# Last stage on token rows: x turned during routing, the gate folded into the expert rows, skips of the extra turns nested

## The reference

```python
g_idx = argmax(h @ w_rg + b_rg); p_group = softmax(...)[g_idx]        # one of 4 groups per token
top_v, top_i = top_k(expert logits of that group, 2)                   # 2 of its 8 experts
gate = p_group * softmax(top_v)                                        # two weights per token
y = (silu(xb @ w_g[e]) * (xb @ w_u[e])) @ w_d[e]                       # D 1024 -> 512 -> 1024, 32 experts
f = sum over the token's two experts of gate * y
x = x_mid + g2 * f                                                     # g2: one factor per feature
return rmsnorm(x, final_norm)                                          # x / sqrt(mean(x^2) + eps) * final_norm
```

## Time and profile before

| | us |
|---|---|
| median of 3 runs | 2240.37 (2237.33 to 2245.26) |
| the profiled execution | 2240.0, its span 2238.2 |
| PE busy | 1921.9 (86%) |
| DVE busy | 886.4 (40%) |
| ACT busy | 378.0 (17%) |
| mean granted clock of PE | 0.923 of full speed |
| DRAM read and written | 359.09 MB, 16.78 MB |

### The profile page before, as it was taken

One profiled execution on the slowest core, in us unless ns is written; L12 is line 12 of the kernel. 1 busy time (PEld: TensorE's weight loads), 2 busy tenths in 40 slices (PEclk: granted clock), 3 DMA queues, 4 the chain that ended last, 5 costly groups with the idle time before them and its releaser, 6 DMA issues. The chain is left out here.

```text
span 2238.2 us, 27833 instructions
## 1 busy us (share of the span) xinstructions
PE 1921.9 (86%) x12018; PEld 997.4 (45%) x12018; DVE 886.4 (40%) x1460; ACT 378.0 (17%) x666; POOL 127.9 (6%) x185
## 2 busy tenths in 40 slices
PE   6999663998699999999898999999996988777882
PEld 3554353886344444444344664456433333332331
DVE  2572575344314888883442004934313000000003
ACT  4212531223102111111012001035012000000001
POOL 0000007230000000000000000010000000000000
PEclk8999875899799999999999999999997999999985
DMA  7452011112211222215641132220445999999973
GB/s 292 158 194 104 0 40 34 27 23 88 91 40 73 75 75 76 75 58 192 275 190 57 57 99 85 75 86 16 159 173 223 425 427 426 426 426 425 425 334 122
DMA packets 72738, 371.84 MB, mean 166 GB/s; under 512 B 33488, under 2 KB 33616, under 8 KB 46240
## 3 DMA queue, kind: packets, MB, share of 16 engines
q1 hardware_dynamic: 68000, 361.21, 41.2%
q0 software_dynamic: 4608, 8.73, 1.0%
HBM read 359.09 MB, written 16.78 MB: 168 GB/s over the span
## 5 line engine op out<-in xcount | busy, mean ns | idle before, releaser
L2467 PE MATMUL psum<-mem 128*64 128x512 f32 x1536 | 364.1, 629 | 53.0 <-DMA mem<-in_w_upe 29.4
L1604 PE MATMUL psum<-mem 128*128 128x512 f32 x704 | 305.7, 596 | 2.0 <-ACT mem L376 2.0
L1331 PE MATMUL psum<-mem 128*128 128x512 f32 x608 | 274.5, 607 | 20.0 <-DMA mem<-in_w_down 14.7
L2467 PEld LDWEIGHTS psum<-mem 128*64 128x64 f32 x1536 | 121.7, 144 | 274.2 <-issue 268.3
L1673 DVE SCALAR_TENSOR_TENSOR mem<-mem 128x512 f32<-128x512 f32 x352 | 237.0, 749 | 0.0
L1837 PE MATMUL psum<-mem 128*128 128x512 f32 x512 | 223.2, 597 | 2.9 <-ACT mem L1851 2.9
L1604 PEld LDWEIGHTS psum<-mem 128*128 128x128 f32 x704 | 134.0, 191 | 173.1 <-issue 171.6
L1331 PEld LDWEIGHTS psum<-mem 128*128 128x128 f32 x608 | 115.2, 193 | 165.5 <-issue 153.5
L568 PE MATMUL psum<-mem 128*128 128x512 f32 (+1 forms) x464 | 167.6, 523 | 2.1 <-ACT mem L376 2.0
L1837 PEld LDWEIGHTS psum<-mem 128*128 128x128 f32 x512 | 97.5, 191 | 125.6 <-issue 123.1
L568 PEld LDWEIGHTS psum<-mem 128*128 128x128 f32 x464 | 88.1, 190 | 80.8 <-issue 73.0
(11 more groups left out here) (342 smaller groups left out, 1995.0 us busy)
## 6 DMA issues: line engine op xcount, KB each, us to landing
mem<-in_w_gate SPq DMA_DIRECT2D x32, 2048.0 KB, 33.3
mem<-in_w_upe SPq DMA_DIRECT2D x32, 2048.0 KB, 32.7
mem<-in_w_downe SPq DMA_DIRECT2D x32, 2048.0 KB, 32.4
mem<-in_ada SPq DMA_DIRECT2D x48, 1024.0 KB, 6.6
mem<-in_w_up SPq DMA_DIRECT2D x22, 1024.0 KB, 4.8
mem<-in_w_in_g SPq DMA_DIRECT2D x12, 1024.0 KB, 4.8
mem<-in_w_down SPq DMA_DIRECT2D x16, 704.0 KB, 4.2
mem<-in_w_in SPq DMA_DIRECT2D x19, 512.0 KB, 3.7
```

The costliest lines, as they stand in the source:

```text
L1331: last = pe.matmul(self.banks[m % 4][:, :], w, self.rhs[:, kt], start=i == 0, stop=i == n - 1, skip_group_check=self.before is not None)
L1604: last = pe.matmul(k.bank[2 * (m % 3) + h2][:, :], w[:, kt, h2], h[:, kt], start=kt == 0, stop=kt == KD - 1)
L2467: last = pe.matmul(bank[halves[h], :], xs[:, kt, halves[h]], pair[h][0][:, kt, cols], start=kt == 0, stop=kt == tiles - 1, skip_group_chec ...
```

## The change

The kernel's output becomes [512 tokens, 1024 features] instead of feature-major, and the constant final_norm is loaded as a [128, 1024] tile of equal rows (final_row) instead of 8 columns of the first constants tile, which shrinks from 860 to 852 columns, so every tile behind it lies 32 bytes lower in each partition.

In routing, PE turns x in place behind the table products, ACT copies it back, and a row of g2 on all partitions (gate_row) is made from eight diagonal tiles:

```diff
             last.then_inc(s["table_mm"], 1)
+            for i in range(8):
+                if i == 2:
+                    pe.wait_ge(s["rows"], 4)
+                if i >= 4:
+                    pe.wait_ge(s["x_rows"], i - 3)
+                for j in range(4):
+                    last = pe.transpose(k.bank[x_banks[i % 4]][:, P * j:P * j + P], halves_of_x[i][:, j], k.c("ident"))
+                last.then_inc(s["x_turned"], 1)
+            pe.wait_ge(s["diagonal"], KD)
+            for kt in range(KD):
+                last = pe.matmul(k.psum[:, 2048 + P * kt:2048 + P * kt + P], k.c("ones"), diagonal[:, kt], start=True, stop=True, skip_group_check=True)
+            last.then_inc(s["gate_mm"], 1)
...
             act.activation(top[1], top[1], ACT.Exp).then_inc(s["exped"], 1)
+            for i in range(8):
+                act.wait_ge(s["x_turned"], i + 1)
+                act.activation(halves_of_x[i], k.bank[x_banks[i % 4]].rearrange("p (j n) -> p j n", j=4), ACT.Copy).then_inc(s["x_rows"], 1)
+            act.wait_ge(s["gate_mm"], 1)
+            act.activation(gate_row, k.psum[:, 2048:3072], ACT.Copy).then_inc(s["gate_row"], 1)
...
             dve.tensor_scalar(table[:, :, 0], found[:, 0], BLANK, None, ADD).then_inc(s["table"], 1)
+            dve.wait_ge(s["turned"], 4)
+            for kt in range(KD):
+                dve.tensor_scalar(diagonal[:, kt], k.c("ident"), gate(kt), None, MUL).then_inc(s["diagonal"], 1)
             dve.wait_ge(s["exped"], 2)
```

In the experts' block the last two matrices are sent together, each in two column halves, after the last send of the others; the last down product runs over kt first and waits per half; the result rows are multiplied by gate_row where they were copied; and all extra turns lie inside one outer test:

```diff
+    def send_last(self, sp):
+        ends = [len(self.stream) - 2 + h for h in range(2)]
+        for i in ends:
+            self.wait_free(sp, i)
+        for part in range(2):
+            cols = slice(2 * D * part, 2 * D * part + 2 * D)
+            for h, i in enumerate(ends):
+                sp.dma_start(self.slots[i % self.SLOTS][:, cols], self.d["w_downe"][N_EXP - 2 + h][:, cols]).then_inc(self.last[part], 16)
...
+    def last_down(pe):
+        n = N_TURN - 1
+        pe.wait_ge(s["hid_t"], n + 1)
+        pe.wait_ge(s["y"], n)
+        pair = [experts.weights("w_downe", n, h)[0] for h in range(2)]
+        for kt in range(4):
+            if kt % 2 == 0:
+                pe.wait_ge(experts.last[kt // 2], 32)
+            for half in range(2):
+                for h in range(2):
+                    last = pe.matmul(k.bank[5 + half][halves[h], :], hid_t[:, kt, halves[h]], pair[h][:, kt, 512 * half:512 * half + 512],
+                                     start=kt == 0, stop=kt == 3, skip_group_check=True)
+        last.then_inc(down_mm, 1)
...
-        dve.tensor_copy(y[n % 2][:, 0:512], k.bank[5][:, :])
-        dve.tensor_copy(y[n % 2][:, 512:1024], k.bank[6][:, :]).then_inc(s["y"], 1)
+        dve.tensor_tensor(y[n % 2][:, 0:512], k.bank[5][:, :], gate_row[:, 0:512], MUL)
+        dve.tensor_tensor(y[n % 2][:, 512:1024], k.bank[6][:, :], gate_row[:, 512:1024], MUL).then_inc(s["y"], 1)
...
-        for o in range(OVER_TURNS):
-            count = eng.value_load(k.over_i[0:1, OVER + 1:OVER + 2], min_val=0, max_val=OVER)
-            with eng.If(count > 2 * o):
-                run(o)
+        any_over = eng.value_load(k.over_i[0:1, OVER + 1:OVER + 2], min_val=0, max_val=OVER)
+        with eng.If(any_over > 0):
+            run(0)
+            for o in range(1, OVER_TURNS):
+                count = eng.value_load(k.over_i[0:1, OVER + 1:OVER + 2], min_val=0, max_val=OVER)
+                with eng.If(count > 2 * o):
+                    run(o)
...
             sp.wait_ge(gathered[0], 16)
-            experts.send(sp, 8, len(experts.stream))
+            experts.send(sp, 8, len(experts.stream) - 2)
+            experts.send_last(sp)
+            sp.dma_start(final_row, k.d["final_row"]).then_inc(s["final_row"], 16)
+            sp.wait_ge(s["final_row"], 16)
```

POOL now waits for the stores of y_rows before the one outer test, and its second chain of eight tests is gone (the waits moved into the extra turns). In the combining block PE has no work; DVE and ACT do, per piece of 128 tokens:

```diff
         def _(act):
             warm_root(k, act)
+            for tt in range(4):
+                act.wait_ge(s["both"], tt + 1)
+                act.activation(squares, yr[:, tt, 0], ACT.Square, accum_out=total[:, tt:tt + 1]).then_inc(s["square"], 1)
+                act.wait_ge(s["square"], tt + 1)
+                act.activation(root[:, tt:tt + 1], total[:, tt:tt + 1], ACT.Sqrt, bias=k.v("eps_norm"), scale=1.0 / D).then_inc(s["root"], 1)
...
+            def add(tt):
                 dve.wait_ge(landed[tt], 16)
+                a, b = yr[:, tt, 0], yr[:, tt, 1]
+                dve.scalar_tensor_tensor(out=eight(a), in0=eight(a), scalar=weights[:, tt, 0:1], in1=x[:, :, P * tt:P * tt + P],
+                                         op0=MUL, op1=ADD).then_inc(s["first"], 1)
                 dve.wait_ge(s["first"], tt + 1)
+                dve.scalar_tensor_tensor(out=a, in0=b, scalar=weights[:, tt, 1:2], in1=a, op0=MUL, op1=ADD).then_inc(s["both"], 1)
+            def scale(tt):
+                dve.wait_ge(s["root"], tt + 1)
+                dve.reciprocal(inverse[:, tt:tt + 1], root[:, tt:tt + 1]).then_inc(s["inverse"], 1)
+                dve.wait_ge(s["inverse"], tt + 1)
+                dve.scalar_tensor_tensor(out=yr[:, tt, 1], in0=yr[:, tt, 0], scalar=inverse[:, tt:tt + 1], in1=final_row,
                                          op0=MUL, op1=MUL).then_inc(s["out"], 1)
+            add(0)
+            for tt in range(1, 4):
+                add(tt)
+                scale(tt - 1)
+            scale(3)
```

More of the change, by code:

```diff
@@ L2148, in _, with route_stage @@
                 dve.tensor_tensor(mix[:, m], gate_a[:, m], gate_b[:, m], ADD).then_inc(s["mix"], 1)
-def route_stage(k, x, spread, gain, shift, experts, h, weights, table, h_dram, w_router, work, at_rows, gather):
+def route_stage(k, x, spread, gain, shift, experts, h, weights, table, h_dram, w_router, work, at_rows, gather, gate, gate_row):
     nc = k.nc
@@ L2384, in __init__ @@
         self.number = {m: i for i, m in enumerate(self.stream)}
-        self.uses = [len(range(i, len(self.stream), self.SLOTS)) for i in range(self.SLOTS)]
+        self.last = [k.sem(f"moe_last_landed_{i}") for i in range(2)]
+        self.uses = [len(range(i, len(self.stream) - 2, self.SLOTS)) for i in range(self.SLOTS)]
     def view(self, slot, name):
@@ L2558, in _ @@
                 scatter(pool, n)
+            for h in range(2):
+                pool.wait_ge(stored[h], 8 * N_TURN)
             def over(o):
@@ L2562, in over @@
                 scatter(pool, N_TURN + o)
+                pool.wait_ge(stored[o % 2], 8 * N_TURN + 16 * (o // 2 + 1))
             over_turns(pool, over)
[L2564 to L2569, removed]
         @block.tensor
@@ L2616, in _, with combine_stage @@
             over_turns(dve, over)
-def combine_stage(k, y_dram, weights, x, gate, at, norm, out):
+def combine_stage(k, y_dram, weights, x, at, work, final_row):
     nc = k.nc
     yr = k.at(at, 8192).rearrange("p (t c w) -> p t c w", t=4, c=2)
-    s = {n: k.sem("combine_" + n) for n in ("first", "both", "turned", "done", "out", "stored")}
+    squares = k.at(work, D)
+    total, root, inverse = (k.small[:, a:a + 4] for a in (0, 4, 8))
+    s = {n: k.sem("combine_" + n) for n in ("first", "both", "square", "root", "inverse", "out", "stored")}
     landed = [k.sem(f"combine_landed_{tt}") for tt in range(4)]
+    eight = lambda x: x.rearrange("p (k n) -> p k n", k=KD)
     with nc.Block("combine") as block:
@@ L2649, in _ @@
                 dve.wait_ge(s["first"], tt + 1)
-                dve.scalar_tensor_tensor(out=yr[:, tt, 0], in0=yr[:, tt, 1], scalar=weights[:, tt, 1:2], in1=yr[:, tt, 0],
-                                         op0=MUL, op1=ADD).then_inc(s["both"], 1)
-            for kt in range(KD):
-                dve.wait_ge(s["turned"], kt + 1)
-                dve.scalar_tensor_tensor(out=x[:, kt], in0=k.bank[kt % 4][:, :], scalar=gate(kt), in1=x[:, kt],
-                                         op0=MUL, op1=ADD).then_inc(s["done"], 1)
```

70 lines of the change are left out of this document (26 added, 44 removed).

## The result

| | before | after |
|---|---|---|
| median, us | 2240.2 (2237.33 to 2245.26, 4 runs) | 2216.26 (2211.84 to 2218.36, 4 runs) |
| profiled execution's span | 2238.2 | 2215.5 |
| ratio of the runs | | 0.9888, 95% interval 0.9864 to 0.9912 |

Faster by 23.9 us; the forecast was 22.6 us, to 2217.8. A second measurement of the same kernel gave 2217.36 (ratio 0.989, 0.9867 to 0.9912).

A forecast was written before the change was run, and what follows sets the result against it. The weight stream at DMA's ceiling was taken to bound the experts' block, leaving its start, its end and the tail to count. 0 - 0.8 - 10.2 - 11.6 = -22.6 us gave 2217.8 for the median, range 2210 to 2226.

The forecast's parts named there:

- Part 1: Routing: transposes of x and gate-row products fit under POOL's second gather; 0 us, between 0 and +4.8.
- Warm start: Start of experts' block: PE's clock already high, turn of x 1.1 us instead of 1.94; -0.8, between 0 and -3.2.
- Part 2: Last down product: with weights in halves PE starts at 2175.45 on the first half; -0.7 us, between 0 and -3.5.
- Part 3: End of experts' block: one outer test around eight bodies; block ends 10.2 us earlier, Part 2's 0.7 included, 7.4 to 12.9.
- Rival B: Gap before combining: what follows the scatter (landing, POOL's closing), not the tests, causes it and stays; 2227.3 us, chance 0.08.
- Part 4: Combining block: without PE, DVE busy to the end, done after 21.7 us instead of 33.3; -11.6, to -6.5.
- The sum: All terms together: -22.6 us against the profiled execution, to 2217.4; for the median of the runs 2217.8.
- A: Routing ends late (+4.8, no warm start, 2223.4 us) or DVE's strided read in combining is dear (2222.9); chance 0.10.
- D: Experts' weight stream loses rate through shifted tiles and 8 KB rows; slower from 6.5%, 2247.1 us; chance 0.04.
- C: PE's clock high through first gate product and end chain too: -2.4 and up to -2.8 more, 2212.6 us; chance 0.12.

The follow-up runs named there:

- a_no_turn: The changed kernel without the turn of x, the diagonals and the gate row in routing; 2219.73 us, run once.
- after_again: The changed kernel run once more, unaltered, beside a neighbour on the same chip; 2217.36 us, ratio 0.989 to the kernel before.
- early_load: The changed kernel with SP's loads of y_rows moved to the end of its list in the experts' block; 2215.34 us, ratio 0.9895 to the kernel before.
- n_pe: The kernel before with one outer test around the extra turns on PE alone, POOL keeping its sixteen tests; 2242.08 us, ratio 1.0005 to before.
- a_triple_gate: The changed kernel with the eight gate-row products in routing made three times over; 2226.71 us, run once.

## Why the prediction was right, point by point

- Part 1, routing for nothing: right. 8.3 us from table products to send, 8.4 before; a_no_turn has 8.1. It was close: in the profiled execution the work overran the gather by 0.3 us, in the other seven traces with it 0.2 to 0.9 were left, and tripled products came out 3.2 us later. PE's clock rose while the transposes ran, but 7.0 us after the table products began and not 4.8: it was low for half of the transposes instead of five. PE's work still took 7.0 us where 7.1 was forecast, because a transpose at the low clock took 0.21 us in this long row (ACT's copies of four come 0.85 apart) and not the 0.25 of the earlier trace rows: two sizes were off and cancelled.
- Warm start, -0.8: right on average (-1.1 over eight traces against five), -1.7 in this trace (12.7 from the block's start to matrix 9's send before, 10.9 after), of which 0.8 is the turn and 0.9 the gate product. The bound of -3.2 was met too: in after_again PE's first gate product ran wholly at the high clock (7.1 us).
- Part 2, -0.7: the mechanism and the size were right only for some executions. In the trace after the last product starts 1.2 earlier after matrix 9's send (451.9 for 453.1); 0.75 of that is the split, the rest lies ahead of it. In four other kernels with the split it brings nothing. The step that failed is "with halves PE starts at 2175.45": it took the copy's time as fixed, and the clock of the down product before it moves the copy by 1.7.
- Part 3, a gap of 9.0 (2182.6 to 2191.6) instead of 18.5: measured 9.5, and the load at 2191.74. PE out of it, POOL last: shown by POOL's DRAIN, the last instruction before the barrier, and by early_load, where SP doesn't wait for it and loads 4.1 sooner behind the scatter. The size was luck, the middle of an interval 5.5 wide: its cheap end had POOL's test right (0.93, measured 0.9) and no term for the DRAIN (2.6), its dear end two fetches, of which POOL's rows show none. The 3.4 put for a fetch stands in none of the rows read ahead (they give 3.2); PE's one branch over all eight bodies took 3.8, hidden beside its last products. The scatter's 2.9 to landing was a median of two; the last took 3.2. One piece of the argument was worthless: the wait's name "PEq", which stands there after the change as well. And the prediction had PE alone as the cause; POOL's sixteen tests end just 1.6 us before PE's, and n_pe shows it.
- Rival B: fallen; taking the tests away brought 9.1 us. The prediction charged PE with at least 2.3 us a test, and the branches there took up to 2.8. The Trainium skill ("Advanced Engine Details and Errata", Control Flow Timing) prices a compare-and-branch at about 108 ns; this case's traces disagree both ways: 45 to 67 ns on the other four engines, 2100 to 2800 ns for six of PE's eight. On POOL it is the whole test, some 0.75 us, that adds up, and the branch is the least of it. The same page of the Trainium skill (ISA Cache) gives lines of 16 KB, which agrees with the blocks fetched.
- Part 4, -11.6: -12.6 in the traces. Two sizes were off: a DVE instruction that doesn't depend on the one before starts 0.05 to 0.07 before that one's end (2197.82 plus 1.28 against a start at 2199.04), where I had put 0.03 to 0.04 of waits, once or twice per piece; and DVE's work took 16.0 where 16.8 was forecast, the first landing 4.76 for 4.87. x read in eight runs costs the same 1.29.
- The sum came out at 22.7 in spans against 22.6, with errors that cancel: routing began 3.4 later in this trace than in that of before (1676.8 for 1673.4, upstream of the change), routing took 1.5 less (1.4 of it ahead of the new work: from the block's start to the table products' end it is 28.5 before and 27.1 after, and 26.9 to 28.6 over all traces, changed or not), the experts' block 1.0 less than forecast and the combining 1.0 less. What the change touches brought 24.6, where 22.6 was forecast; that the total fits to 0.1 is luck.
- Rivals A and D: fallen for this kernel; the stream's rate is 426 GB/s to the digit. C occurred in part, in after_again and a_triple_gate.

## What to carry to other kernels

Skips of code are work: here most tests in front of PE's long bodies took 3.3 to 3.6 us each, 2.1 to 2.8 of it the branch, and on engines with short bodies a test still cost 0.7 to 0.8 for the most part. Since every engine walks its own chain, shorten the chains on all of them and look in the trace which engine's closing instruction comes last. Work laid under a wait is free only to its end; look up how much of the cover is left, and what state (here PE's clock) the work leaves behind. Where one engine bounds a block, its neighbours are not free help: measure whether the two slow each other.

## What the hardware showed unexpectedly

- DVE's two-source instruction of 1024 fp32 columns takes 1.28 us alone and 3.2 beside a POOL product of the same size, which itself takes 3.35 (an estimate of 2.1 alone, from its 768-column form at 1.54); ACT's square beside both stays at 1.06.
- POOL needs 4.2 us from the last scatter's landing (2187.5) to the next block's start, although it has no work left: 0.9 for one test, 0.4 more to the DRAIN and 2.6 in it. In before the DRAIN took 2.5 as well, 9 us after the scatter had landed (2188.6), so it isn't the landing that it waits for. Another engine that waits for the same semaphore goes on at once: in early_load the scatter lands at 2186.06 and SP sends at 2186.14.
- PE's branches over skipped bodies took 0.2 to 2.8 us (median 2.6), the other engines' 0.045 to 0.067.
- Instruction lists that are the same up to routing reach it over a spread of 13.8 us (1669.5 to 1683.3) between executions.
